# Where a transpose is done: TensorE turns replaced by 32-wide VectorE turns and DMA moves in a two-layer decoder trunk

## The reference

```python
h = x
for layer in range(DEPTH):                       # DEPTH = 2
    if layer == N_A_LAYERS:                      # before the second layer
        kb, vb, kmean = shared_kv(h, kv_norm, w_kv)
    h = h + 0.5 * swiglu(rmsnorm(h, ffn1_norm[layer]), ffn1_w_in[layer], ffn1_w_out[layer])
    hn = rmsnorm(h, mix_norm[layer])
    if layer < N_A_LAYERS:
        h = h + s5_mixer(hn, ...)
    else:
        h = h + moba_attention(hn, w_q[j], w_o[j], kb, vb, kmean)
    h = h + 0.5 * swiglu(rmsnorm(h, ffn2_norm[layer]), ffn2_w_in[layer], ffn2_w_out[layer])
return rmsnorm(h, final_norm)

def swiglu(x, w_in, w_out):                      # w_in: 1024 x 5632, w_out: 2816 x 1024
    g, u = jnp.split(x @ w_in, 2, axis=-1)
    return (jax.nn.silu(g) * u) @ w_out
```

## Time and profile before

| | |
|---|---|
| median of 3 runs | 970.87 us (969.37 to 973.48) |
| the profiled execution | 969.86 us |
| its span in the profile | 967.7 us |
| PE busy | 955.9 us (99%) |
| PE weight loads busy | 790.2 us (82%) |
| DVE busy | 597.8 us (62%) |
| ACT busy | 499.8 us (52%) |
| POOL busy | 189.5 us (20%) |
| DMA | 169.35 MB in 47557 packets, the main queue at 54.5% of 16 engines |

### The profile page before, as it was taken

How to read it: one execution, slowest core, us unless ns; L and a number is a source line. 1 busy time by engine, 2 the same in 40 slices (tenths; PEclk the granted TensorE clock), 3 DMA queues, 4 the chain that set the end, 5 groups by cost and what they waited for, 6 DMA issues and landing times.

```text
span 967.7 us, 15102 instructions
## 1 busy us (share of the span) xinstructions
PE 955.9 (99%) x6110; PEld 790.2 (82%) x6110; DVE 597.8 (62%) x744; ACT 499.8 (52%) x711; POOL 189.5 (20%) x235
## 2 busy tenths in 40 slices
PE   9999999999999999999999999999999999999997
PEld 7888888788788888888888888888888888888886
DVE  5565779889765554656555555555557555656544
ACT  7554544576555454545544454554458454545441
POOL 4899999800000000000000000000060000000000
PEclk9999999999999999999999999999999999999999
DMA  9766555520455655565566666656651366555551
GB/s 347 269 184 197 181 174 174 175 69 5 142 187 193 194 178 194 184 208 183 166 198 196 193 177 196 191 177 195 188 182 45 111 198 193 186 187 192 179 169 43
DMA packets 47557, 169.35 MB, mean 175 GB/s; under 512 B 5505, under 2 KB 5505, under 8 KB 47489
## 3 DMA queue, kind: packets, MB, share of 16 engines
q1 hardware_dynamic: 47056, 167.79, 54.5%
q10 hardware_dynamic: 432, 0.61, 0.2%
HBM read 167.33 MB, written 1.05 MB: 174 GB/s over the span
## 4 chain that ended last, share of the span: by engine, by line
PE 88%; DVE 8%; issue 2%; ACT 1%; DMA 1%; SPq 0%; POOLq 0%; POOL 0%; DVEq 0%; ACTq 0%
PE ps L1252 85%; DVE w_lo L931 2%; PE ps L1257 2%; DVE scan L1158 1%; DVE tmp L1087 1%; PE ps L1284 1%; DMA raw<-in_in 1%; DVE rot_b L1165 1%; DVE rot_a L1145 1%; DVE rot_b L1147 1%; ACT w_hi L652 0%; DVE rot_in L1154 0%; DVE states L1172 0%; PE ps L1297 0%; ACT pr L881 0%
## 5 line engine op out<-in xcount | busy, mean ns | idle before, releaser
L931 DVE TENSOR_TENSOR w_lo<-raw,w_hi 128x1024 fp32r<-128x1024 f32 x311 | 399.7, 1289 | 307.0 <-ACT w_hi L652 305.7
L652 ACT ACTIVATE w_hi<-raw 128x1024 fp32r<-128x1024 f32 x311 | 328.4, 1059 | 305.9 <-PE ps L1252 303.2
L1252 PE MATMUL ps<-w_hi,x_hi 128*128 128x512 f32 x896 | 352.4, 393 | 0.9 <-DVE w_lo L931 0.6
L1252 PE MATMUL ps<-w_hi,x_lo 128*128 128x512 f32 x896 | 349.3, 390 | 0.0
L1252 PE MATMUL ps<-w_lo,x_hi 128*128 128x512 f32 x896 | 349.2, 390 | 0.0
L1252 PEld LDWEIGHTS ps<-w_hi,x_hi 128*128 128x128 f32 x896 | 168.4, 188 | 37.2 <-DVE w_lo L931 1.4
L1252 PEld LDWEIGHTS ps<-w_hi,x_lo 128*128 128x128 f32 x896 | 168.3, 188 | 35.2
L1252 PEld LDWEIGHTS ps<-w_lo,x_hi 128*128 128x128 f32 x896 | 168.5, 188 | 34.0
L1252 PE MATMUL ps<-w_hi,hid_hi 128*128 128x512 f32 x352 | 138.1, 392 | 1.0 <-DVE w_lo L931 1.0
L1252 PE MATMUL ps<-w_lo,hid_hi 128*128 128x512 f32 x352 | 137.2, 390 | 0.0
L1252 PE MATMUL ps<-w_hi,hid_lo 128*128 128x512 f32 x352 | 137.2, 390 | 0.0
(11 more groups left out here) (151 smaller groups left out, 599.6 us busy)
## 6 DMA issues: line engine op xcount, KB each, us to landing
raw<-in_in SPq DMA_DIRECT2D x175, 512.0 KB, 4.3
raw<-in_out SPq DMA_DIRECT2D x88, 512.0 KB, 3.4
raw<-in_glu SPq DMA_DIRECT2D x16, 512.0 KB, 4.3
raw<-in_k SPq DMA_DIRECT2D x8, 512.0 KB, 4.4
raw<-in_v SPq DMA_DIRECT2D x8, 512.0 KB, 4.1
raw<-in_q SPq DMA_DIRECT2D x8, 512.0 KB, 4.4
raw<-in_o SPq DMA_DIRECT2D x8, 512.0 KB, 4.0
xt<-in_xt SPq DMA_DIRECT2D x4, 256.0 KB, 5.6
```

What stands on the lines that cost most here:

```text
L652: act.activation(w_hi[:, gu % WS, :], raw[:, gu % RAW, :], ACT.Copy)\
L931: dve.tensor_tensor(w_lo[:, gu % WS, :], raw[:, gu % RAW, :], w_hi[:, gu % WS, :].bitcast(F32), ALU.subtract)\
L1252: return pe.matmul(o, w, x, start=start, stop=stop, skip_group_check=True)
```

## The change

In the in phases 3, 7 and 11 (feed-forwards two to four) the hidden values are no longer turned by PE. DVE transposes every 32 x 32 square of a block in place, in SBUF, and SP then issues DMAs that carry the squares to their places in `hid_lo`. A DMA takes 32 partitions to 32 others; a pair of blocks needs 4 x 4 = 16 of them. ACT makes the high part from `hid_lo` and DVE the low part in place. The same is done for both blocks of k and for the first half of h (chunks 0 and 1) after phases 4 and 8, on a tile `sheet` that takes the place of `kq`; k's second block uses half of `q_sb`. Phase 0, the other chunks of h, q and the attention's own turns stay on PE. The code, abridged:

```diff
+Q = 32
+QS = P // Q
+MOVE_BEHIND = 8
+SHEETS = [(4, 0), (5, 0), (5, 1), (8, 0)]
+BY_ROWS = [(2, 0), (2, 1), (2, 2), (2, 3), (4, 2), (4, 3), (8, 2), (8, 3), (10, 0), (10, 1), (10, 2), (10, 3)]
+MOVED = 16 * QS * QS
...
 def batch_behind(p, phases, b):
-    if p.name == "in" and b in BATCHES[1:]:
+    if p.n == 0 and b in BATCHES[1:]:
         return p, range(b - BATCH, b)
-    if p.name == "out" and b == 0:
+    if p.n == 1 and b == 0:
...
+def pair_end(p, b):
+    return min(b // 2 * 2 + 1, p.blocks - 1)
...
+def high_behind(p, phases, b, j):
+    if p.n < 2:
+        return high_batch(p, phases, b, j)
+    if p.name == "in" and b >= 4 and b % 2 == 0 and j < 2:
+        return [(p, b - 4 + j)]
+    if p.name == "out" and b == 0 and j in (4, 5, 8):
+        f = phases[p.n - 1]
+        return [(f, f.blocks - 7 + j if j < 8 else f.blocks - 1)]
+    return []
...
 def low_behind(p, phases, b, j):
+    if p.name == "in" and b >= 4 and b % 2 == 0 and 1 <= j < 3:
+        return [(p, b - 5 + j)]
+    if p.name == "out" and b == 0 and j in (5, 6, 9):
+        f = phases[p.n - 1]
+        return [(f, f.blocks - 8 + j if j < 9 else f.blocks - 1)]
...
+        def pieces(p, b, n, q, c):
+            return pair_of(pair_number(p, b))[Q * q:Q * q + Q, 0:n]\
+                .rearrange("p b t (a c x) -> p c (b t a) x", a=2, x=Q)[:, c]
+        def places(b, n, q, c):
+            return hid_lo[Q * c:Q * c + Q, 2 * b:2 * (b + n), :].bitcast(F32)\
+                .rearrange("p i (t q x) -> p q (i t) x", t=TT, x=Q)[:, q]
...
+            def move_hidden(p, b, q):
+                k, n = pair_number(p, b), pair_end(p, b) + 1 - b
+                sp.wait_ge(hid_squares, p.hid0 - phases[0].blocks + b + n)
+                for c in range(QS):
+                    sp.dma_start(places(b, n, q, c), pieces(p, b, n, q, c)).then_inc(hid_moved[k % 2], 16)
+            def move_sheet(n, b, q):
+                sp.wait_ge(sheet_squares, SHEETS.index((n, b)) + 1)
+                for c in range(QS):
+                    sp.dma_start(sheet_places(n, b, q, c), sheet_pieces(n, b, q, c))\
+                      .then_inc(sheet_moved, 16)
+            sheet_moves = {phases[n].unit0 + (b + 1) * phases[n].upb + MOVE_BEHIND + q: (n, b, q)
+                           for n, b in SHEETS for q in range(QS)}
+            moves = {p.unit0 + (pair_end(p, b) + 1) * p.upb + MOVE_BEHIND + q: (p, b, q)
+                     for p in phases if p.name == "in" and p.n for b in range(0, p.blocks, 2)
+                     for q in range(QS)}
...
             for gu in range(10, len(units)):
                 load(gu)
+                if gu in moves:
+                    move_hidden(*moves[gu])
+                if gu in sheet_moves:
+                    move_sheet(*sheet_moves[gu])
...
             def high_hidden(p, b):
+                k = pair_number(p, b)
+                act.wait_ge(hid_moved[k % 2], MOVED * (k // 2 + 1))
+                act.activation(hid_hi[:, 2 * b:2 * b + 2, :], hid_lo[:, 2 * b:2 * b + 2, :].bitcast(F32),
+                               ACT.Copy).then_inc(hid_hi_done, 1)
...
             def gated(p, b):
+                    elif p.name == "in":
+                        k = pair_number(p, b)
+                        if k >= 2:
+                            dve.wait_ge(hid_moved[k % 2], MOVED * (k // 2))
+                        dve.scalar_tensor_tensor(tile_of(p, b, q), halved(ps[:, bank(gb, q), HB:NB]),
+                                                 rs[:, q:q + 1], halved(act_out[:, q, :]),
                                                  ALU.mult, ALU.mult).then_inc(drained, 1)
...
+                if p.name == "in" and p.n:
+                    dve.wait_ge(drained, p.drained0 + TT * (b + 1))
+                    whole = prod_of(p, b).rearrange("p t x -> p (t x)")
+                    dve.transpose(whole, whole).then_inc(hid_squares, 1)
...
             def low_hidden(p, b):
+                dve.wait_ge(hid_hi_done, p.hid0 + b + 1)
+                part = hid_lo[:, 2 * b:2 * b + 2, :]
+                dve.tensor_tensor(part, part.bitcast(F32), hid_hi[:, 2 * b:2 * b + 2, :].bitcast(F32),
+                                  ALU.subtract).then_inc(hid_ready, 1)
...
+            def turned_sheet(p, b):
+                dve.wait_ge(kq_drained, p.kq0 + TT * (b + 1))
+                whole = sheet_at(p.n, b).rearrange("p i t x -> p (i t x)")
+                dve.transpose(whole, whole).then_inc(sheet_squares, 1)
+            def turned_h(p):
+                dve.wait_ge(drained, p.drained0 + TT)
+                if p.n == 8:
+                    dve.wait_ge(sheet_moved, MOVED * 3)
+                for q in range(TT):
+                    ins = dve.transpose(sheet[:, :, q, :],
+                                        h[:, q, 0:NB].rearrange("p (i x) -> p i x", x=P))
+                    if q:
+                        ins.then_inc(sheet_squares, 1)
...
+        def high_unit(n, c):
+            return 1 if (n, c) in BY_ROWS else 8 + c
```

More of the change, by code:

```diff
@@ L118, in batch_behind, with high_batch @@
     return p, range(0)
-def high_behind(p, phases, b, j):
-    if p.name == "in" and b in BATCHES[1:] and j >= 2:
+def high_batch(p, phases, b, j):
+    if p.n == 0 and b in BATCHES[1:] and j >= 2:
         first = b - BATCH + 2 * (j - 2)
         return [(p, first), (p, first + 1)]
-    if p.name == "out" and b == 0 and j in (2, 3):
+    if p.n == 1 and b == 0 and j in (2, 3):
         f = phases[p.n - 1]
@@ L130, in high_behind, with low_batch, pair_number @@
     return []
-def low_behind(p, phases, b, j):
[L135 to L140, removed]
+def low_batch(p, phases, b, j):
+    if p.n == 0 and b in BATCHES[1:] and j == 3:
+        return [(p, b - BATCH)]
+    if p.n == 0 and b - 1 in BATCHES[1:] and j >= 1:
+        return [(p, b - 1 - BATCH + j)]
+    if p.n == 1 and b == 0 and 3 <= j < 3 + phases[p.n - 1].blocks - BATCHES[-1]:
+        return [(phases[p.n - 1], BATCHES[-1] + j - 3)]
+    return []
+def pair_end(p, b):
+    return min(b // 2 * 2 + 1, p.blocks - 1)
+def pair_number(p, b):
+    return (p.hid0 // p.blocks - 1) * ((p.blocks + 1) // 2) + b // 2
+def high_behind(p, phases, b, j):
[6 more added lines that the diff above has]
+        return [(f, f.blocks - 7 + j if j < 8 else f.blocks - 1)]
+    return []
+def low_behind(p, phases, b, j):
+    if p.n < 2:
+        return low_batch(p, phases, b, j)
+    if p.name == "in" and b >= 4 and b % 2 == 0 and 1 <= j < 3:
[3 more added lines that the diff above has]
+        return [(f, f.blocks - 8 + j if j < 9 else f.blocks - 1)]
     return []
@@ L304, in trunk @@
         hid_turned = sem("hid_turned")
+        hid_squares = sem("hid_squares")
+        hid_moved = [sem(f"hid_moved{i}") for i in range(2)]
         hid_hi_done = sem("hid_hi_done")
@@ L391, in trunk @@
             sq_at[n] = total, parts
-        turned = {nc_: i for i, nc_ in enumerate((n, c) for n in (2, 4, 8, 10) for c in range(DT // 2))}
+        turned = {at: t for t, at in enumerate(BY_ROWS)}
         NORM = {0: 1, 3: 2, 5: 3, 6: 3, 7: 3, 9: 4, 11: 5}
@@ L694, in high_x @@
             def high_x(n, c):
-                act.wait_ge(h_turned, turned[n, c] + 1)
+                if (n, c) in BY_ROWS:
+                    act.wait_ge(h_turned, turned[n, c] + 1)
+                else:
+                    act.wait_ge(sheet_moved, MOVED * (sheet_of(n, c) + 1))
                 for gain, buf in X_OF[n]:
@@ L719, in after @@
                     squares(p, b, HB)
-                    high_x(p.n, b)
+                for c in turned_now(p, b, j):
+                    high_x(p.n, c)
                 if p.name in ("out", "o") and j == 0:
                     squares(p, b, NB)
-                if p.n in (4, 8, 10) and j == 1:
-                    for c in (2 * b, 2 * b + 1):
-                        high_x(p.n, c)
                 if p.name in ("k", "q") and j == 0:
@@ L957, in low_turned @@
                     for i in range(2):
-                        low_x(ps[:, TA + turned[n, c] % 2, i * TOK:i * TOK + TOK],
-                              (x_hi[buf], x_lo[buf]), 2 * c + i, gain)
+                        low_x(turned_x(n, c, i), (x_hi[buf], x_lo[buf]), 2 * c + i, gain)
             def gated(p, b):
@@ L1290, in turn_kq @@
                 for c in range(2):
[L1291 removed]
+                    t = 2 * b + c
                     if t >= 2:
@@ L1295, in turn_kq @@
                         for q in range(TT):
[L1296 removed]
                             last = pe.transpose(ps[:, KT + c, i * TOK + q * P:i * TOK + q * P + P],
[L1298 removed]
+                                                sheet[:, 2 * c + i, q, :], ident[:, :])
                     last.then_inc(kq_turned, 1)
             def after(p, b, j):
[L1303 to L1308 removed]
+                cs = {"glu": (b,), "out": (2 * b, 2 * b + 1), "o": (2 * b, 2 * b + 1)}.get(p.name, ())
+                for c in cs:
+                    if j == 0 and (p.n, c) in BY_ROWS:
```

(4 more changed lines are left out.)

141 lines of the change are left out of this document (82 added, 59 removed).

## The result

The changed kernel takes 956.62 us (median of 4, 955.31 to 957.59), the one before beside it 971.82 (median of 4). The ratio is 0.984, with a 95% interval from 0.982 to 0.987: faster by 15.2 us. Forecast were 956.5 us and a faster kernel.

A forecast was written before the change was run, and what follows sets the result against it. PE was taken as the bound, holding 88% of the chain. 969.86 - 15.0 = 954.9 us, 955.9 with the median 1.0 above, plus half a microsecond for joints: 956.5 us; range 953 to 972.

The forecast's parts named there:

- What is removed: PE's turns in phases 3, 7 and 11 (11.5 us) and of h and k (3.6 us), together 15.0 us saved.
- VectorE: New transposes of hidden values, h and k on DVE: 28 us of work, none of it exposed.
- SP: 352 more DMAs to issue; SP falls 1.2 us behind in the four units after a pair and catches up at once.
- The DMA engines: Runs of 128 bytes beside the weight loads: 20 ns each, 5 us a pair, share 0.84, hidden.
- the line through two packet sizes: Price of a 128-byte run on the DMA engines, from the 2 KB and 4 KB packets: 15 ns.
- The limit of 44 ns for a run: DMA engines beside the weight loads: from 44 ns a run the loads starve.
- two estimates from the Trainium skill: Price of a 128-byte run on the DMA engines: 8 ns by descriptor cost, some 97 ns by a 19-fold difference.
- Lateness: Moves landing before ACT asks for the pair: 12 us against 2.6 + 4.3, exposed 0; ACT's lead forgives another 5 us.
- The turns weren't covered: Rival on PE: the turns were covered anyway, no change, 970.9 us; chance 0.04.
- SP was the nearer: Rival that SP becomes the bound: at 1.42 us an issue, +4.4 us a pair, 1046 us; chance 0.04.
- the DMA engines 0.14: Rival: DMA engines become the bound at weights' landing in phases 3, 7 and 11; 1040 us at 60 ns; chance 0.14.
- The half microsecond for the joints: Small waits at the joints, half a microsecond added to the sum.

The follow-up runs named there:

- dve_thrice: Changed kernel with VectorE transposing every block of hidden values of feed-forwards two to four three times in place instead of once; 955.50 us.
- issues_32: Changed kernel with each move of hidden values issued as two DMAs of 128 runs instead of one of 256; 1057.43 us.
- extra_x2: Changed kernel with one more DMA of 1024 runs of 128 bytes, awaited only at the end, behind each of four loads after a pair's moves; 956.48 us.
- behind_13: Changed kernel with the moves five units later in SP's list (MOVE_BEHIND 13 for 8); 1053.47 us.
- behind_11: Changed kernel with the moves three units later in SP's list (MOVE_BEHIND 11 for 8); 963.20 us.
- hidden_back: Changed kernel with hidden values of feed-forwards two to four turned by TensorE again, the sheets of k and h still moved; 966.48 us.
- runs_64: Changed kernel with each move of hidden values issued as two DMAs of 256 runs of 64 bytes instead of one of 256 runs of 128; 1077.27 us.
- extra_x5: Changed kernel with two more DMAs of 2048 runs of 64 bytes behind each of the four loads after a pair's moves; 1105.51 us.
- behind_12: Changed kernel with the moves four units later in SP's list (MOVE_BEHIND 12 for 8); 1000.18 us.

## Why the prediction held, point by point

- **What is removed.** Reckoned 15.0 us from distances between starts, 13.1 from the chain's pieces. The stretch shows 675.2 - 659.8 = 15.4, in its parts 11.8 and 3.7 for 11.5 and 3.6, and all of it is busy time of TensorE (668.1 to 652.7). Starts were the right measure.
- **VectorE.** Transposes 0.71 us (0.69 taken) and covered; 42 us more are covered as well (dve_thrice).
- **SP.** Here the reading was wrong and the sum nearly right by luck. The prediction has 0.43 us for an issue of 128 runs and 0.65 for 256, as if the price went by the runs. A move takes 0.59 to 0.61 us with either (issues_32), so the 0.65 held, but not for its 256 runs, and a load right behind moves takes 0.60 and not 0.43. The four units behind a pair cost SP 3.2 us each and not 3.0, so it falls 1.9 us behind, and the quarters start at SP's own pace.
- **The DMA engines.** 15 ns by the line through two packet sizes, 20 taken, 13 to 14 measured: the windows give 13 and 14, and the main queue's share, 0.632 x 955.8 against 0.545 x 967.7 us, times 16 engines over 89,600 packets more, gives 14. (84,000 were forecast; the other 5,632 are 16 for each of the 352 new DMAs.) The share of the stage is 0.75, where 0.84 was reckoned. The limit of 44 ns for a run wasn't reached, and twice the runs still pass, at a share of 0.94 (extra_x2). Of the prediction's two estimates from the Trainium skill, 8 and 97 ns, the measured one is near the first. But it was worked out from a section of the Trainium skill's page DMA: Bandwidth & Descriptors, Why small descriptors are slow (HBM only), that excepts transfers from SBUF to SBUF, and the moves are such. So it is no confirmation: they cost 13 to 14 ns where their bytes alone would be 5.
- **Lateness.** The margin was reckoned for the out phase, 12 - 6.9 = 5.1 us. There it is 0.7 to 2.1 us for the half pair and 1.3 to 4.2 for the last full one. The sum left out that SP gets to the last quarter late: it falls behind with each quarter, and at a phase's end two sets of moves follow each other. That the 5.2 us of the view agree with it is chance, for that pair is in the middle of a phase. No wait came of it, but with less to spare than the prediction says. ScalarE's lead is worth about 4.4 us, for the 5 given.
- **Rivals.** The turns weren't covered, as the chain had said. Of the two that end slower, SP was the nearer: it was given 0.04, with a price of 1.42 us an issue from the full queue, and the DMA engines 0.14. The runs turn that around: twice the issues cost 101 us, twice the runs none.
- **The half microsecond for the joints** did not appear: ScalarE has no wait for hidden values, and TensorE's idle time in the stretch is 7.0 us, 7.1 before. The forecast of 956.5 us also met a median with the part ahead of phase 3 in it, whose length varies by 3 us; that it came out within 0.1 us of 956.62 is luck.
- **What the prediction had no term for** is the clock. It priced its slower rivals by idle time alone. In the slowed runs a quarter of the loss is busy time at a lower granted clock (24.5 of 101.7 us in issues_32, 27.0 of 97.2 in behind_13).

## What to carry to other kernels

Where TensorE sets the end, a transpose is worth the distance between the starts of the matmuls around it, and DMA moves of 32 x 32 squares can take it over if three budgets hold per period: SP's issues, the engines' runs, and the landing against the step that reads them. Count issues first, for a move costs SP the same with 128 runs as with 256. Larger ones pay only so far: behind a DMA of 1024 runs the next issue takes longer. Check the margin where two sets of moves meet and not only in the middle of a phase. Count a pause of TensorE at more than its length. And look who else is in the stage: the same move that was free beside an idle GpSimd lost 5.5 us beside a busy one.

## What the runs showed that I had not expected

- What an issue costs SP depends on what it is and what went before. After the first 60 us a weight load took 0.33 us by itself, 0.43 right behind another load and 0.60 right behind a move (medians in the changed kernel), for the same 128 runs. A move took 0.59 to 0.61 us with 128 or 256 runs, and 0.59 even after a pause. So the 0.43 of the earlier trace rows was no price of 128 runs, and the early loads weren't cheap ones. Why a move costs more, and makes the load behind it cost more, is open.
- The part ahead of phase 3 comes in two lengths, whatever the kernel. The chain starts phase 3 at 292.5, 293.2, 293.2, 293.6 and 293.0 us in the profiles of before, behind_11, behind_13, issues_32 and dve_thrice, and at 296.1, 295.9, 295.7, 295.2, 295.2 and 295.1 in those of the changed kernel, hidden_back, runs_64, extra_x2, extra_x5 and behind_12. The changed kernel and its edits do the same work up to there. In the six long ones GpSimd waits 2.46 us for a table of VectorE's at the end of the S5 preparation, in the five short ones not. That an interplay of these two engines decides it is argued, not shown. It is why the profiled spans differ by 11.9 us and the stretches by 15.4.
